# Output projection by token groups of 352, with the merging and the second norm done group by group

## Chip, core and metric

One core of one Trainium2 chip runs the whole program. The metric is the device time of one execution in microseconds (us). Three timed runs of the kernel before gave 2089.18, 2090.16 and 2091.87 us, so 2090.16 us is the median. The engines are TensorE (PE, matrix products), VectorE (DVE), ScalarE (ACT), GpSimd (POOL), and SyncE (SP), which only issues transfers (DMAs). Each engine takes its instructions in the order of its own program; they meet through semaphores.

## The reference

One step of a decoder layer with D = 1024 on 1024 prompt tokens and 8 x 4 sample tokens (1056 in all), in float32:

```python
h = rmsnorm(x, norm_mix_w) * (1.0 + sc1) + sh1
z = h @ w_in + b_in                       # 8 sections of 1024 columns
q_raw, f_raw, i_raw, og_raw, glu_a, glu_b, gate_a, gate_b = jnp.split(z, IN_SPLITS, axis=-1)
o_a, s_new = hgrn2_branch(q_raw, f_raw, i_raw, og_raw, lb, hgrn_norm_w, s0)
o_b, buf_new = conformer_conv_branch(glu_a, glu_b, buf, ...)   # ends in a layer norm and silu
merged = jnp.concatenate([sigmoid(gate_a) * o_a, sigmoid(gate_b) * o_b], axis=-1) @ w_out
x = x + g1 * merged
h2 = rmsnorm(x, norm_ffn_w) * (1.0 + sc2) + sh2
gg, uu = jnp.split(h2 @ w_ffn_in, 2, axis=-1)
x = x + g2 * ((jax.nn.silu(gg) * uu) @ w_ffn_out)
y = rmsnorm(x, norm_final_w)
```

## The kernel before

Activations lie with features on the 128 partitions and the 1056 tokens along a row: 8 feature tiles of [128, 1056]. The tokens form three groups of 352 (G = 3, GW = 352). A float32 product is made of three products of rounded parts: high x high, high x low, low x high. So each weight block of [128, 8 x 128] is loaded by SP (`load_block`, L434), rounded by ACT (`hi`, L1621), and its rest is formed by DVE or POOL (`low`, L1145 and L1888). Raw, high and low parts have two buffers each. SP may load block b when block b-2 is split (`w_split`); ACT rounds block b when PE has finished block b-2 (`block_done`).

The stages around the change:

- The last eight projection tiles (gate b, ZT + 0 to 7), each one block by three groups, 72 matmuls. Between their matmuls PE places the fills of `LAST` (five slots per tile): the recurrence of the last head, the mean of the convolution (`mu`), the token sums of its squares (`lnss`), and the layer norm's row of factors (`lnr`). ACT squares the centred tiles (L1755), POOL adds the squares up (L1998), ACT takes the root, DVE scales (L1373), ACT applies weight and bias (L1762, L1763), and DVE multiplies for the silu (L1412).
- Merging. The 16 tiles of the merged activations come back from DRAM as whole rows of 1056 tokens (`mraw`, four buffers). The eight of the second half are multiplied with the convolution's output by POOL (L2005); then ACT rounds (L1776) and DVE forms the rest (L1416). The rests lie where the projection's input lay, so they begin when the last gate tile is done.
- Output projection: 8 tiles of 128 output features, each of 2 blocks by 3 groups, 144 matmuls, 16 blocks in all. After a tile DVE adds the gated result to the residual (`tab`, two buffers, loaded by SP at L621), ACT squares the new x into the same buffer (L1826), and DVE adds the square to `ysum` (L1465).
- Second norm: token sums over all tokens (L913), root, rows, then shift and split for the first group by DVE, ACT and POOL together (L1120, L1650, L2013), and for the other two by POOL (L2023 to L2035) beside the FFN.
- FFN: for each group 22 hidden tiles of 2 blocks of 24 matmuls, then 8 output tiles of 66 matmuls.

The order in which SP issues the loads in a pair of output tiles is: residual, residual, then four weight blocks.

## Time and profile before

| | |
|---|---|
| median of three runs | 2090.16 us |
| profiled execution | 2090.47 us, span 2088.8 us |
| PE busy | 1992.8 us, 95% of the span, 15928 matmuls |
| DVE / ACT / POOL busy | 1252.0 / 659.3 / 262.4 us |
| mean granted TensorE clock | 0.974 of full speed |
| the chain that ended last | PE 86%, DVE 6%, POOL 3%, DMA 2%, ACT 2% |

A busy share is an average over stages that have different limits. The rows below are therefore taken by stage: each names a stretch, in us from the start of the span. In a timeline row the columns are the start, the duration, the engine, the line of the kernel, the operation with its tiles and shapes, the count, and in brackets how long the engine had been idle and what released it. The granted clock is a share of 2.4 GHz, so 0.50 is the lower level of 1.2 GHz.

### The profile page before, as it was taken

How to read it: one execution, taken by the hardware profiler on the slowest of the kernel's cores; microseconds unless marked ns; L12 is line 12 of the kernel's file. 1: busy time of each engine (PE TensorE's matmuls, PEld its weight loads, DVE VectorE, ACT ScalarE, POOL GpSimd, SP SyncE). 2: the span in 40 equal slices, each digit the busy share in tenths (PEclk: the TensorE clock that was granted, in tenths of full speed). 3: DMA queues.
4: the chain of work that ended last, by engine and by line, in shares of the span. 5: the costliest groups of instructions: out<-in, count | busy, mean ns of one | idle time of the engine just before them, and what ended most of it. 6: DMA issues, size and time to landing. Idle time of an engine off the chain costs nothing.

```text
span 2088.8 us, 39144 instructions
## 1 busy us (share of the span) xinstructions
PE 1992.8 (95%) x15928; PEld 1904.4 (91%) x15928; DVE 1252.0 (60%) x1667; ACT 659.3 (32%) x1001; POOL 262.4 (13%) x216
## 2 busy tenths in 40 slices
PE   7699999999999999999968997999999999999997
PEld 3599999999999999998868997999999999999997
DVE  2776979797878787876364123555445544455544
ACT  2421322222232323132452113555333333333332
POOL 0420010101010101022333222930000000000000
PEclk9799999999999999999979997999999999999998
DMA  7422222222222222222262211444444544445442
GB/s 248 159 74 55 73 75 73 75 74 76 73 75 73 76 72 76 64 81 83 73 207 93 71 61 31 133 139 140 132 141 142 149 132 137 134 142 150 140 138 91
DMA packets 368857, 220.72 MB, mean 106 GB/s; under 512 B 15208, under 2 KB 360200, under 8 KB 368705
## 3 DMA queue, kind: packets, MB, share of 16 engines
q1 hardware_dynamic: 368720, 218.77, 35.4%
q8 instruction: 102, 1.67, 0.3%
q14 instruction: 35, 0.28, 0.0%
HBM read 195.49 MB, written 24.11 MB: 105 GB/s over the span
## 4 chain that ended last, share of the span: by engine, by line
PE 86%; DVE 6%; POOL 3%; DMA 2%; ACT 2%; issue 1%; SPq 0%; DVEq 0%; ACTq 0%; POOLq 0%
PE Z L772 76%; PE R L797 2%; PE R L719 1%; PE R L850 1%; POOL mraw L2005 1%; DMA ada_w<-in_w_ada_dram 1%; PE R L803 1%; POOL ysum L1998 1%; PE R L895 1%; DVE ta L1310 1%; PE R L882 1%; PE R L875 1%; DVE x L1514 1%; DVE k L1174 1%; PE R L884 1%
## 5 line engine op out<-in xcount | busy, mean ns | idle before, releaser
L772 PE MATMUL Z<-h_hi,w_hi 128*128 128x352 f32 x2592 | 701.9, 335 | 24.0 <-POOL h_lo L1902 15.9
L772 PE MATMUL Z<-h_hi,w_lo 128*128 128x352 f32 x2592 | 675.7, 325 | 0.0
L772 PE MATMUL Z<-h_lo,w_hi 128*128 128x352 f32 x2592 | 674.5, 324 | 0.0
L1621 ACT ACTIVATE w_hi<-w_raw 128x1024 fp32r<-128x1024 f32 (+1 forms) x284 | 295.8, 1042 | 997.9 <-PE Z L772 966.9
L1145 DVE TENSOR_TENSOR w_lo<-w_raw,w_hi 128x1024 fp32r<-128x1024 f32 (+1 forms) x260 | 316.8, 1219 | 313.9 <-ACT w_hi L1621 306.2
L772 PEld LDWEIGHTS Z<-h_hi,w_hi 128*128 128x128 f32 x2592 | 455.0, 191 | 51.0 <-issue 33.5
L772 PEld LDWEIGHTS Z<-h_hi,w_lo 128*128 128x128 f32 x2592 | 465.7, 190 | 0.0
L772 PEld LDWEIGHTS Z<-h_lo,w_hi 128*128 128x128 f32 x2592 | 465.0, 190 | 0.0
L1293 DVE SCALAR_TENSOR_TENSOR yb<-up,vec,yb 128x1024 f32 (+1 forms) x240 | 308.3, 1284 | 29.8 <-DVE yb L1293 3.7
L772 PE MATMUL Z<-act_hi,w_hi 128*128 128x352 f32 x528 | 170.2, 322 | 0.0
L772 PE MATMUL Z<-act_hi,w_lo 128*128 128x352 f32 x528 | 169.5, 321 | 0.0
L772 PE MATMUL Z<-act_lo,w_hi 128*128 128x352 f32 x528 | 169.3, 321 | 0.0
L1888 POOL TENSOR_TENSOR w_lo<-w_raw,w_hi 128x1024 fp32r<-128x1024 f32 x24 | 59.2, 2468 | 373.7 <-ACT w_hi L1621 373.7
L1963 POOL TENSOR_TENSOR gate<-ta,tb 128x1056 f32<-128x1056 f32 x8 | 20.8, 2599 | 659.0 <-ACT ta L1683 659.0
L772 PEld LDWEIGHTS Z<-act_hi,w_lo 128*128 128x128 f32 x528 | 99.3, 188 | 0.0
L772 PEld LDWEIGHTS Z<-act_lo,w_hi 128*128 128x128 f32 x528 | 99.2, 188 | 0.0
L772 PEld LDWEIGHTS Z<-act_hi,w_hi 128*128 128x128 f32 x528 | 99.1, 188 | 0.0
L1545 DVE TENSOR_TENSOR tb<-ta,Z 128x352 f32<-128x352 f32 x66 | 34.4, 521 | 68.3 <-PE Z L772 67.7
L1173 DVE TENSOR_TENSOR qd<-qd,tot 128x512 f32<-128x512 f32 (+1 forms) x48 | 33.1, 690 | 43.1 <-PE R L850 41.8
L772 PE MATMUL Z<-m_hi_a,w_hi 128*128 128x352 f32 x192 | 43.5, 336 | 12.2 <-DVE m_lo_a L1416 11.8
L772 PE MATMUL Z<-m_hi_b,w_hi 128*128 128x352 f32 x192 | 43.1, 333 | 9.7 <-DVE m_lo_b L1416 9.7
L1704 ACT ACTIVATE osq<-R 128x128 f32<-128x128 f32 x80 | 21.0, 275 | 92.7 <-PE R L884 70.4
(282 smaller groups left out, 2069.8 us busy)
## 6 DMA issues: line engine op xcount, KB each, us to landing
w_raw<-in_w_ffn_in_dram SPq DMA_DIRECT2D x132, 512.0 KB, 3.8
w_raw<-in_w_in_dram SPq DMA_DIRECT2D x64, 512.0 KB, 5.0
w_raw<-in_w_ffn_out_dram SPq DMA_DIRECT2D x48, 512.0 KB, 4.1
aw<-in_w_ada_dram SPq DMA_DIRECT2D x32, 512.0 KB, 4.3
w_raw<-in_w_ffn_out_dram SPq DMA_DIRECT2D x24, 384.0 KB, 3.3
mraw<-merged_scratch SPq DMA_DIRECT2D x16, 528.0 KB, 4.3
ada_w<-in_w_ada_dram SPq DMA_DIRECT2D x8, 1024.0 KB, 7.6
w_raw<-in_w_out_dram SPq DMA_DIRECT2D x16, 512.0 KB, 4.0
```

The lines of the kernel that those rows point to most:

```text
L719: last = mm(R[n % 2][0:NSEQ, 0:2 * P], ct[:, kt, 0:NSEQ], ada_w[n % 2][:, kt, :], start=kt == 0, stop=kt == NJ - 1)
L772: last = mm(out, w[:, kt, :], x(kt, g), start=first and kt == 0 and m == 0, stop=last_block and kt == n - 1 and m == 2)
L797: return transpose(out, in_, ident[0:m, 0:m])
L803: last = mm(bank[group:group + 32, ADA_COL:ADA_COL + P], ct[:, kt, :], aw[:, kt, :], start=kt < 4, stop=kt >= 4)
L850: last = mm(bank[p:p + BAND, c * w:(c + 1) * w], k[:, t:t + BAND], halves(qd[:, t:t + BAND], 1 << lv, 1), start=True, stop=True)
L1145: st.tell(V.tensor_tensor(w_lo[b.par][:, 0:n, :], w_raw[b.par][:, 0:n, :], w_hi[b.par][:, 0:n, :].bitcast(F32), ALU.subtract), w_split, b. ...
L1173: st.do(V.tensor_tensor(late, late, pairs[:, :, 0:1].to_broadcast(shape), ALU.mult))
L1293: ins = V.scalar_tensor_tensor(yp, xp, w, yp, ALU.mult, ALU.add)
L1545: st.tell(V.tensor_tensor(a, sg, Z[t.par][:, 1, 0:GW], ALU.mult), *zfree(t))
L1621: A(w_hi[b.par][:, 0:n, :], w_raw[b.par][:, 0:n, :], ACT.Copy).then_inc(w_hi_ready, 1)
L1704: last = A(osq[:, col + i, :], bank[:, i * P:(i + 1) * P], ACT.Square, accum_out=oss[:, col + i:col + i + 1])
L1888: st.tell(Q.tensor_tensor(w_lo[b.par][:, :, :], w_raw[b.par][:, :, :], w_hi[b.par][:, :, :].bitcast(F32), ALU.subtract), w_split, b.v + 1)
```

## The change

The output projection runs group by group: 24 tiles of 48 matmuls (group outermost) instead of 8 of 144. Each group loads all 16 weight blocks again, so there are 48 blocks. DVE forms the rest of every block from the third on, POOL no longer does. Merging goes by pieces of 352 tokens: group 0 lands in free places of `x2` and is merged before the projection, groups 1 and 2 pass through seven small buffers while the tiles run (`M_AT`). The squares of a tile are added on DVE one tile later (`x2_add`), and its residual buffer is reloaded after that. The second norm's sums and rows are made per group beside the next group's tiles (for the last group beside the first FFN tiles); shift and split are POOL's for all three groups. Both roots become a power of -0.5 on POOL. The layer norm's squares start two tiles earlier, DVE adds them up instead of POOL, and scaling, affine and silu go in pieces of 352 tokens. The diff is cut to what the steps below need; what the removed lines did is told above.

```diff
-LAST = ([("rec", n) for n in range(N_LV)] + [("mu", n) for n in range(3)] + [("rec", n) for n in range(N_LV, N_OS)]
-        + [("lnss", 0)] + [("rec", N_OS)] + [("lnr", n) for n in range(3)]
-        + [("rec", n) for n in range(N_OS + 1, NFILL)])
+LAST = ([("rec", n) for n in range(N_LV)] + [("mu", n) for n in range(3)] + [("rec", n) for n in range(N_LV, N_KV0)]
+        + [("lnss", 0), ("rec", N_KV0), ("rec", N_KV1), ("lnr", 0), ("rec", N_O0), ("rec", N_O1), ("lnr", 1),
+           ("rec", N_OS), ("lnr", 2)] + [("rec", n) for n in range(N_KVS0, NFILL)])
+LAST_PAUSE = 29
...
+M2 = 2 * NJ
+MBUF = 7
+M_FIRST = (6, 7, 12, 13, 4, 5, 14, 15, 10, 11, 8, 9, 0, 1, 2, 3)
+M_AT = {0: range(16, 19), 1: range(19, 22), 2: range(22, 25), 3: range(25, 28), 4: range(28, 30), 5: range(30, 32),
+        8: range(32, 34), 9: range(34, 36), 10: range(36, 38), 11: range(38, 40), 14: range(40, 44),
+        15: range(44, 48)}
...
+    def merged_at(c):
+        g, m = divmod(c, M2)
+        raw = x2[:, M_FIRST[c] // 2, group(1 + M_FIRST[c] % 2)] if g == 0 else mbuf[(c - M2) % MBUF][:, :]
+        return raw, m_hi[m // NJ][:, m % NJ, group(g)], m_lo[m // NJ][:, m % NJ, group(g)]
+    def m_landed(c):
+        return (m_first[c], 16) if c < M2 else (m_loaded[(c - M2) % MBUF], 16 * ((c - M2) // MBUF + 1))
...
+            def load_m(c):
+                g, m = divmod(c, M2)
+                if g:
+                    wait(sp, m_split, c - MBUF + 1)
+                elif m >= NJ:
+                    sp.wait_ge(gb_stored[m % 2], 16 * ((m - NJ) // 2 + 1))
+                sp.dma_start(merged_at(c)[0], merged[m, :, group(g)]).then_inc(m_landed(c)[0], 16)
...
+                if j == 5:
+                    sp.wait_ge(m_stored, 16 * (NJ - 1))
+                    sp.wait_ge(centred, NJ)
+                    sp.wait_ge(fill_done, rec7(N_KTS).n + 1)
+                    for c in range(4):
+                        load_m(c)
...
+            def load_out(b):
+                load_block(Idx(Z_OUT + b), wout_v[:, b % 2 * 8:b % 2 * 8 + 8, b // 2 % NJ * P:(b // 2 % NJ + 1) * P])
+            def load_residual(n):
+                wait(sp, x2_summed, n - 1)
+                sp.dma_start(tab[n % 2][:, 0:GW], xt_dram[n % NJ, :, group(n // NJ)]).then_inc(xr_loaded[n % 2], 16)
+            load_out(0)
+            store_gate(5)
+            load_out(1)
             store_o(h7, rec7(N_OT2))
+            for c in (6, 8, 9):
+                load_m(c)
+            store_gate(6)
             sp.wait_ge(m_stored, 16 * NJ)
+            for c in (7, 10, 11):
+                load_m(c)
+            sp.wait_ge(ln_done, G * NJ)
+            for c in (12, 13):
+                load_m(c)
+            load_out(2)
+            load_out(3)
+            store_gate(7)
             for i in range(2):
                 sp.wait_ge(gb_stored[i], 16 * NJ // 2)
+            ahead = iter(range(M2, G * M2))
+            for c in range(MBUF):
+                load_m(next(ahead))
+            sp.wait_ge(m_prod, NJ)
+            load_residual(0)
+            load_residual(1)
+            for n in range(G * NJ):
+                if n < G * NJ - 2:
+                    load_out(2 * n + 4)
+                    load_residual(n + 2)
+                    load_out(2 * n + 5)
+                for _ in M_AT.get(n, ()):
+                    c = next(ahead, None)
+                    if c is not None:
+                        load_m(c)
...
+            def x2_fill(g, n):
+                bank = small(Idx(R_X2 + 2 * g + n))
+                if n == 0:
+                    pe.wait_ge(x2_summed, NJ * (g + 1))
+                    last = token_sums(bank, ysum[:, group(g)], GW)
+                else:
+                    pe.wait_ge(x2_recip, g + 1)
+                    last = rows_of(bank, 0, GW, rs9)
+                last.then_inc(fill_done, 1)
+            for n in range(G * NJ):
+                g, j = divmod(n, NJ)
+                pe.wait_ge(*zfree(Idx(Z_OUT + n - 2)))
                 for kk in range(2):
...
+                    beside = g and j == kk == 1 or g and j == 0 and kk == 1
+                    products(Idx(Z_OUT + 2 * n + kk), [Z[n % 2][:, 0, 0:GW]], NJ,
+                             lambda kt, _: m_hi[kk][:, kt, group(g)], lambda kt, _: m_lo[kk][:, kt, group(g)],
+                             kk == 0, kk == 1, (lambda: x2_fill(g - 1, j)) if beside else None, (5,) if beside else (),
+                             (lambda kt: pe.wait_ge(m_split, M2 * g + NJ * kk + kt + 1)) if j == 0 else None)
...
+            def add_square(j):
+                if j < 1:
+                    return
+                dve.wait_ge(ln_squared, j + 1)
                 st.settle()
...
+                st.tell(V.tensor_tensor(ysum[:, :], ysum[:, :], (v, f)[j % 2][:, :], ALU.add), ln_added, j)
...
+            after = {("rec", N_O0): (4, 0), ("rec", N_O1): (4, 0), ("rec", N_OS): (8, 0), ("lnr", 2): (0, 4),
+                     ("rec", N_KVS0): (4, 0), ("rec", N_KVS1): (4, 0), ("rec", N_OT0): (0, 4), ("rec", N_OT1): (0, 4)}
...
+            def x2_add(n):
+                dve.wait_ge(x2_squared, n + 1)
+                st.tell(V.tensor_tensor(ysum[:, group(n // NJ)], ysum[:, group(n // NJ)], tab[n % 2][:, 0:GW], ALU.add),
+                        x2_summed, n + 1)
+            dve.wait_ge(w_split, Z_OUT + 2)
+            for n in range(G * NJ):
+                g, j = divmod(n, NJ)
+                low(Idx(Z_OUT + 2 * n + 2))
+                if n:
+                    st.settle()
+                    x2_add(n - 1)
+                for c in M_AT.get(n, ()):
+                    merged_low(c)
+                low(Idx(Z_OUT + 2 * n + 3))
+                if g and j < 2:
+                    x2_evac(g - 1, j)
+                t = Idx(Z_OUT + n)
+                dve.wait_ge(block_done, Z_OUT + 2 * n + 2)
+                dve.wait_ge(xr_loaded[n % 2], (n // 2 + 1) * 16)
+                a, b = g * GW, (g + 1) * GW
+                todo = gated_add(x2[:, j, a:b], tab[n % 2][:, 0:GW], Z[n % 2][:, 0, 0:GW], G1, j, a, b)
+                for m, make in enumerate(todo):
+                    st.settle()
+                    ins = make()
+                    st.do(ins) if m < len(todo) - 1 else st.tell(ins, *zfree(t))
...
-                    act.wait_ge(*evac(Idx(REC7 + LAST_AT[("lnss", 0)])))
-                    root(NINE, ln_root)
...
+            for c in range(M2 - 2, M2):
+                merged_hi(c)
+            for n in range(G * NJ):
+                hi(Idx(Z_OUT + 2 * n + 2))
+                for c in M_AT.get(n, ()):
+                    merged_hi(c)
+                hi(Idx(Z_OUT + 2 * n + 3))
+                act.wait_ge(*zfree(Idx(Z_OUT + n)))
+                A(tab[n % 2][:, 0:GW], x2[:, n % NJ, group(n // NJ)], ACT.Square).then_inc(x2_squared, 1)
...
+                if j == 3:
+                    pool.wait_ge(*evac(Idx(REC7 + LAST_AT[("lnss", 0)])))
+                    st.do(Q.tensor_tensor(rs9[:, 0:NC], ms9[:, 0:NC], mhalf[:, 0:NC], ALU.pow))
+                    st.tell(Q.tensor_tensor(rs9[0:TS, NC:NC + 1], ms9[0:TS, NC:NC + 1], mhalf[0:TS, NC:NC + 1],
+                                            ALU.pow), ln_recip, 1)
...
+            pool.wait_ge(ln_done, G * NJ)
+            for c in range(NJ, M2 - 1):
+                gated(c)
             low(Idx(Z_OUT + 1))
...
+            gated(M2 - 1)
+            gated_group(1)
...
+            for g in range(G):
+                root(g)
+                pool.wait_ge(*evac(Idx(R_X2 + 2 * g + 1)))
...
+                if g == 0:
+                    gated_group(2)
```

## Rows read from the trace of the kernel before

**Rows 1.** The table by stage: length, busy PE, PEld, DVE, ACT, POOL; clock, DMA, GB/s

```profile
960.00:1000.00 40.00, 40.00 (x402) 38.38 (x401) 19.67 (x36) 15.80 (x27) 17.56 (x8) 1.00 0.42 134
...
1040.00:1080.00 40.00, 28.19 (x143) 26.73 (x142) 23.60 (x22) 26.09 (x24) 4.90 (x2) 0.79 0.48 162
1080.00:1120.00 40.00, 29.95 (x158) 27.32 (x157) 30.02 (x16) 11.77 (x11) 30.30 (x10) 0.91 0.54 175
...
1280.00:1320.00 40.00, 33.91 (x161) 31.54 (x161) 21.32 (x30) 18.62 (x30) 24.95 (x26) 0.68 0.23 67
```

**Rows 2.** Waits of PE, 900 to 1400: us in total, times, longest

```profile
PE Z L772 <- DVE m_lo_a L1416: 11.8, 4, 5.6
PE Z L772 <- DVE m_lo_b L1416: 9.7, 7, 2.0
PE Z L772 <- POOL h_lo L2013: 5.1, 4, 1.3
PE R L913 <- DVE ysum L1465: 4.9, 1, 4.9
PE R L913 <- POOL ysum L1998: 4.7, 1, 4.7
```

**Rows 3.** PE in slices of 5: length, busy, clock, DMA, GB/s

```profile
950.00:955.00 5.00, 2.61 (x69) 0.57 0.00 0
...
1000.00:1005.00 5.00, 0.36 (x3) 1.00 0.00 0
1005.00:1010.00 5.00, 4.93 (x23) 0.53 0.00 0
1010.00:1015.00 5.00, 5.00 (x52) 0.78 0.00 0
...
1300.00:1305.00 5.00, 5.00 (x17) 0.50 0.02 5
```

**Rows 4.** The chain that ended last: start, us, what

```profile
1110.96 163.43 PE Z L772 x1008
...
1299.94 50.16 PE Z L772 x297
```

**Rows 5.** Timeline of ACT in the FFN, two blocks in a row

```profile
1342.04 1.06 ACT L1621 ACTIVATE w_hi<-w_raw 128x1024 fp32r<-128x1024 f32 x1 [2.37 <-PE Z L772]
...
1345.85 1.06 ACT L1621 ACTIVATE w_hi<-w_raw 128x1024 fp32r<-128x1024 f32 x1 [2.40 <-PE Z L772]
```

**Rows 6.** Timeline of DVE in the same stretch

```profile
1340.46 1.27 DVE L1548 TENSOR_TENSOR act_lo<-tb,act_hi 128x352 f32 x1
1343.14 1.23 DVE L1145 TENSOR_TENSOR w_lo<-w_raw,w_hi 128x1024 fp32r<-128x1024 f32 x1 [1.40 <-ACT w_hi L1621]
```

**Rows 7.** Timeline of DVE at an FFN output tile

```profile
1491.52 0.58 DVE L1439 SCALAR_TENSOR_TENSOR x<-Z,mod,x 128x352 f32 x1 [0.34 <-DVE w_lo L1145]
1492.77 0.53 DVE L1590 TENSOR_TENSOR ysum<-ysum,tb 128x352 f32<-128x352 f32 x1 [0.67 <-ACT tb L1869]
```

**Rows 8.** Timeline of ACT at the same FFN output tile

```profile
1492.24 0.50 ACT L1869 ACTIVATE tb<-x 128x352 f32 x1 [2.32 <-DVE x L1439]
1492.67 0.85 ACT L1621 ACTIVATE w_hi<-w_raw 128x768 fp32r<-128x768 f32 x1
```

**Rows 9.** Timeline of DVE around the output projection

```profile
1055.98 1.26 DVE L1416 TENSOR_TENSOR m_lo_a<-mraw,m_hi_a 128x1056 fp32r<-128x1056 f32 x1 [5.04 <-PE Z L772]
...
1139.42 1.26 DVE L1465 TENSOR_TENSOR ysum<-ysum,tb 128x1056 f32<-128x1056 f32 x1 [1.27 <-ACT tb L1826]
```

**Rows 10.** Timeline of SP in the output projection

```profile
1140.87 0.35 SPq L621 DMA_DIRECT2D tb<-xt_scratch  x1
```

**Rows 11.** Line L434 alone, 1110 to 1290: its weight loads' time to landing

```profile
DMA to landing us min/median/max: 3.7/4.0/5.0
```

**Rows 12.** Timeline of POOL: the eight merging products, a product of 352

```profile
1080.86 25.39 POOL L2005 TENSOR_TENSOR mraw<-mraw,yb 128x1056 f32<-128x1056 f32 x8 [7.04 <-DMA mraw<-merged_scratch]
...
1301.02 0.93 POOL L2023 TENSOR_TENSOR h2buf<-x,ysum 128x352 f32<-128x352 f32 x1 [0.17 <-POOL h_lo L2013]
```

More of the change, by code:

```diff
@@ L295, in program @@
     eps = low_place("eps", [P, 1])
+    mhalf = low_place("mhalf", [P, NC + 1])
+    h2buf = low_place("h2buf", [P, GW])
     vblk = at("vblk", [TS, NS, P], F32, r.where["ktok"])
-    mraw = [at(f"mraw{i}", [P, T], F32, r.where[n]) for i, n in enumerate(("up", "gate", "tot", "O"))]
+    mbuf = [at(f"mbuf{i}", [P, GW], F32, low_place.where["otok"] + i * GW * 4) for i in range(MBUF)]
+    assert MBUF * GW * 4 <= (2 * NC + 4) * P * 4
     murow = at("murow", [P, T], F32, r.where["up"])
@@ L1383, in _ @@
                             centre(j)
-                    for j in (next(to_scale, None), next(to_scale, None)):
-                        if j is not None:
-                            scale(j)
-                    continue
-                dve.wait_ge(fill_done, fill.n + 1)
+                    if m >= N_LV:
+                        for j in (next(to_add, None),):
+                            if j is not None:
+                                add_square(j - 1)
+                else:
+                    dve.wait_ge(fill_done, fill.n + 1)
                 if kind == "mu":
@@ L1489, in x2_rows @@
-            def x2_rows(n):
-                fill = R_X2 + 1 + n
-                t0, w = ROW_PARTS[n]
-                dve.wait_ge(fill_done, fill + 1)
-                st.tell(V.tensor_copy(ysum[:, t0:t0 + w], R[fill % 2][:, 0:w]), *evac(Idx(fill)))
-            x2_rows(0)
-            st.settle()
-            for j in range(NJ):
-                wait(dve, h2_ready, j - 1)
-                modulate(tab[j % 2][:, 0:GW], x2[:, j, 0:GW], ysum[:, 0:GW], j, SH2, 0, GW, h2_full, j + 1)
-                if j in (1, 2):
-                    x2_rows(j)
+            THREE = ((P, slice(0, 2)), (GW - 2 * P, slice(2, 3)))
@@ L1815, in _ @@
-            gate_b(NJ - 1)
-            hi(Idx(Z_OUT + 1))
-            for m in range(3, 2 * NJ):
-                merged_hi(m)
-            with act.Fori(0, NJ // 2) as i:
-                for n in range(2):
-                    ft = Idx(n, i, 2)
-                    for kk in range(2):
-                        hi(Idx(Z_OUT + 2 + 2 * n + kk, i, 4))
-                    act.wait_ge(*zfree(Idx(Z_OUT + n, i, 2)))
-                    A(tab[n][:, :], at_head(x2, ft.v), ACT.Square).then_inc(x2_squared, 1)
@@ new lines, in gated, with gated_group @@
+            def gated(c):
+                g, m = divmod(c, M2)
+                j = m - NJ
+                if c < NJ + 6 or g:
+                    pool.wait_ge(*m_landed(c))
+                    gate = merged_at(c)[0]
+                else:
+                    pool.wait_ge(*zfree(Idx(ZT + j)))
+                    gate = tab[j % 2][:, 0:GW]
+                st.tell(Q.tensor_tensor(merged_at(c)[0], gate, yb[:, j, group(g)], ALU.mult), m_prod, NJ * g + j + 1)
+            def gated_group(g):
+                for j in range(NJ):
+                    gated(M2 * g + NJ + j)
```

300 lines of the change are left out of this document (107 added, 193 removed).

## The prediction

> **What bounds the kernel now.** The table by stage shows TensorE (PE) filled almost everywhere except between the last projection tiles and the FFN [rows 1]: in 1040 to 1120 it is busy 58 of 80 us at clocks of 0.79 and 0.91, and in 1280 to 1320 at 0.68. Its waits name the causes [rows 2]: 4.7 us for POOL's sums of squares of the layer norm (the norm's token sums, L913), 11.8 and 9.7 us for the low halves of the merged tiles, 4.9 and 5.1 us for the second norm. Each pause also costs clock [rows 3]: after the one that ends at 1005 the clock is 0.53, then 0.78, which loses 0.47 x 5 + 0.22 x 5 = 3.4 us. The chain of work then has one unbroken piece, 1008 matmuls in 163.4 us [rows 4], 162 ns each: the output projection, with nothing waiting. Here the change works, so this piece has to be read from the side of its feeders: how long does a weight block need to be loaded, rounded (ACT, L1621) and split (DVE, L1145), and in what order do the engines do it?
>
> One block of 24 matmuls takes 3.81 us, the distance of two roundings that wait for PE [rows 5]. A rounding starts when the block two before it is done, its product is used 1.10 us later by DVE, which takes 1.23 [rows 6]: 2.33 us from start of rounding to block ready. Call this R.
>
> **The change, part by part.**
>
> *Layer norm.* The seven adds leave POOL for DVE and the squares come two tiles earlier. The wait of 4.7 us and the 3.4 us of slow clock go: 8.1. The adds cost DVE 1.26 each (an add of that width, [rows 9]), 8.8 in all; DVE was busy only half of 960 to 1000 [rows 1], so of the bounds 0 and 8.8 I take 1. The root as a power on POOL is in no row: 8 columns, between nothing and the 3.17 us of a product of 1056 columns (25.39 / 8, [rows 12]); some 6 us of two other fills lie between the sums and its first reader, so it is hidden. Gain 7.
>
> *Start of the output projection.* Let t = 0 be the end of the last projection tile (1055.98 before, when DVE starts the first low half, [rows 9]). The normalised group 0 is ready about then, but POOL does seven products of 352 columns (3.17 / 3 = 1.06 each), then the split of block 1, then the eighth; block 1 runs at about 8 to 12. The split of block 3 stands in DVE's order behind the low halves of three tiles of group 1, and SP issues their loads only after the last gate tile is stored (about 14). So block 3 runs at about 20 and block 4 is split at about 25 (20 to 30).
>
> *Output projection.* Matmuls: the same 1152, at 3.81 / 24 = 159 instead of 162 ns. But the weights are now loaded, rounded and split three times (48 blocks instead of 16), two blocks in each 7.62 us. What was hidden before by tiles of 23 us must now fit 7.62. Follow one tile. L is the moment when block 2n+4 is split.
> 1. DVE then adds the squares of tile n: 0.03 + 0.53 = 0.56 [rows 7].
> 2. SP's next instruction is the residual load of tile n+2, which waits for that add, because it overwrites the same buffer; **the load of block 2n+5 is queued behind it**. SP starts 0.19 after the add (1139.42 + 1.26 to 1140.87, [rows 9, 10]); the residual's issue holds it about 0.40 (0.35 there).
> 3. The weight load lands 3.7 to 5.0 us after issue, median 4.0 [rows 11]; with 176 KB of residual ahead of it 4.2.
> 4. Rounding and split: R = 2.33. Block 2n+5 is ready at L + 0.56 + 0.19 + 0.40 + 4.2 + 2.33 = L + 7.68, while PE finished block 2n+4 at L + 3.81. PE is idle 3.9 us.
> 5. Only now DVE, in order, evacuates tile n+1: 0.05 + 0.58 [rows 7]. ACT, in order, squares it: 0.14 after, and takes its next rounding 0.43 later [rows 8]. That rounding is block 2n+6: again R. So block 2n+6 is split at L + 7.68 + 0.63 + 0.57 + 2.33 = L + 11.2.
>
> The period is 11.2 us for 7.62 us of matmuls. It repeats for all loads that SP queues this way: from block 4 to block 46, 21 periods, and the last tile ends 7.68 + 3.81 = 11.5 after. POOL adds to it: the second norm of groups 0 and 1 (16 steps of four operations) and 16 products now run beside this chain, some 75 us at 0.93 each [rows 12], or 7 tiles. A DVE operation of 352 columns beside POOL took 1.27 where 0.53 is normal [rows 6, 7]. Between 0 and 0.74 for each of the four DVE operations of a tile, I take 0.3: 7 x 4 x 0.3 = 8, and 2 for the two small operations per tile that the sample tokens add in the last group. Sum: 25 + 21 x 11.2 + 11.5 + 10 = 282 us. Before: 1110.96 + 163.43 - 1055.98 = 218 [rows 4, 9]. **Loss 63.**
>
> The Trainium skill (SBUF — State Buffer, the engine ports) says that a DVE operation with two SBUF inputs and a GpSimd operation exclude each other for a whole instruction. The 1.27 us beside 0.53 agrees in kind. If each of the four waited for a whole 0.93, that part would be 7 x 4 x 0.93 = 26 instead of 8, and the time 18 us longer; nothing else here uses it.
>
> *Second norm.* From the end of the projection (1274.4) to 1299.94 [rows 4] is 25.5; the slice 1300 to 1305 did 17 matmuls where 31 fit [rows 3], 2.2 more; but 21 matmuls of the first block were done in between (3.3). So 24.4 is lost today. In the new kernel groups 0 and 1 are normed beside the projection, and the last group's sums and rows (about 1.4 us of PE) beside FFN tiles. What is late next, the first FFN weights, is loaded without a residual in front. Gain 23.
>
> Sum against the profiled execution (2090.47, span 2088.8; it lies 0.3 above the median of the runs): 2090.5 - 7 + 63 - 23 = 2124.
>
> **The rivals.**
> *A, no queueing (faster).* If the odd block's load is not held up, PE never waits: 25 + 22 x 7.62 = 193 instead of 218, so -25 - 7 - 23 = -55: **2035**. For it: before, weight loads were always early. Against: the order in SP's text, and step 2 has no way round. It would need the block ready 3.9 us sooner.
> *B, half of the chain (faster).* Step 4 holds, step 5 does not, because the evacuation of tile n+1 or its square is out of the way. Then block 2n+4 is ready R after block 2n+2, and PE loses 1.2 per tile: period 8.8; 25 + 21 x 8.8 + 9 + 5 = 224, +6 - 30 = -24: **2066**. It decides from a period under 9.9, where loss and gains meet. Against: ACT and DVE take instructions in order and the new text has both in front of the next rounding.
> *C, the clock (much slower).* A pause of PE inside 950 to 955 left a clock of 0.57 [rows 3], and the new kernel has 3.9 us of pause in each tile. At half clock a block takes 7.6, which still fits into the 7.68 until the next is ready, so one slow block in two is free. If both were slow, the period would be 15.2: 25 + 21 x 15.2 + 15 + 10 = 369, +151 - 30 = +121: **2211**. Against: with both slow PE has no pause left, and the clock then comes back, as it did by 1015. The Trainium skill (TensorE: Matmul & The Clock Gate, HAM oscillation) warns of just this pattern, a wait for data before each group of matmuls and a clock that falls every time.
>
> **How the numbers follow.** Forecast 0.80: the order is in the text, the durations in rows. A 0.05, B 0.06, C 0.05, and 0.04 for other sizes around zero. The bounds of the forecast: landing 3.7, start 20, no contention: 20 + 21 x 10.7 + 11 = 256, +38 - 30 gives 2098. Landing 5.0, start 30, contention 15, adds not hidden (norm gains nothing): 30 + 21 x 12 + 12.3 + 15 = 309, +91 - 23 gives 2158. These ends would have to coincide, so the range is 2100 to 2154. A measurement of this kernel can tell about 0.2% (4 us) from no change: faster 0.11, same 0.03, slower 0.86.
>
> **What would show it.** In the new profile: PE waiting for w_lo of the odd blocks, twenty-odd times some 3.5 to 4 us; ACT's rounding waiting for the weight load there, and its even roundings waiting for DVE; tiles 11 us apart; a granted clock below 1 in the projection; no wait at the layer norm's sums and almost none before the FFN. If tiles are 7.6 apart, step 2 is wrong; if 8.8, step 5; if the projection is as forecast and the time is not, the gains are.

## The result and the profile after

The changed kernel takes 2127.85 us (median of 4 runs, 2124.66 to 2131.97); the kernel before, on the same chip, 2089.67 us (4 runs, 2088.92 to 2091.87). The ratio is 1.0193, 95% interval 1.0176 to 1.0210: slower by 1.9%. The forecast was 2124.0 in a range of 2100 to 2154. The profiled execution of after is the slowest of its four, 2131.97 us with a span of 2130.3 and a mean granted clock of 0.974.

The table by stage of after, columns as in [rows 1] (length, busy PE, PEld, DVE, ACT, POOL with the numbers of instructions, then clock, DMA share, GB/s):

```profile
960.00:1000.00 40.00, 38.29 (x313) 36.90 (x306) 26.61 (x44) 12.56 (x23) 7.18 (x4) 1.00 0.43 134
1040.00:1080.00 40.00, 26.67 (x136) 23.54 (x134) 25.61 (x32) 17.86 (x33) 14.36 (x10) 0.91 0.53 163
...
1120.00:1160.00 40.00, 31.27 (x170) 30.41 (x169) 13.55 (x18) 8.56 (x13) 0.00 (x0) 0.87 0.48 137
...
1320.00:1360.00 40.00, 33.58 (x202) 33.17 (x203) 19.01 (x31) 12.03 (x16) 1.88 (x3) 0.96 0.41 118
```

The projection, which was the unbroken piece of [rows 4], now has PE busy 31 of 40 us (1120 to 1160), while every feeder is idle more than half of that stretch. Nobody is full: a sign of a chain of waits. The waits of PE from 900 to 1400 (total, times, longest; compare [rows 2]):

```profile
PE Z L804 <- DVE w_lo L1174: 68.2, 24, 5.5
PE Z L804 <- DVE m_lo_a L1422: 4.7, 7, 2.2
```

Neither the layer norm's sums nor the second norm appears any more; the low halves of weight blocks do, some once per tile. Who keeps them late (waits of SP's queue and of ACT, 1070 to 1360):

```profile
SPq L642 <- DVE ysum L1506: 211.0, 22, 12.4
...
ACT w_hi L1655 <- DMA w_raw<-in_w_out_dram: 133.5, 21, 8.7
```

SP stands 211 us in front of the residual load (L642). One tile, from the chain of work that ended last, 1153 to 1166 (start, us, what):

```profile
1153.40 1.24 DVE w_lo L1174
...
1154.66 0.54 DVE ysum L1506
...
1155.21 0.34 SPq L642
...
1155.59 4.22 DMA w_raw<-in_w_out_dram
...
1159.84 1.07 ACT w_hi L1655
...
1160.93 1.23 DVE w_lo L1174
...
1162.42 0.59 DVE x L1476
...
1163.44 1.05 ACT w_hi L1655
...
1164.52 1.24 DVE w_lo L1174
```

This is the prediction's chain, step by step: split of the even block, add (0.54), residual issue, landing 4.22, rounding and split, evacuation, rounding and split. From one even block's split to the next it is 11.12 us (1153.40 to 1164.52), forecast 11.2; the odd block is 7.53 after the even one (1160.93), forecast 7.68.

The whole difference of the two profiled executions, 41.5 us, splits at three moments. The first is DVE's first write of the convolution's mean (`murow`: before at 934.51, after at 930.00). The second is DVE's first low half of the merged tiles [rows 9], in after:

```profile
1043.22 8.85 DVE L1422 TENSOR_TENSOR m_lo_a<-x,m_hi_a 128x352 fp32r<-128x352 f32 x8 [0.18 <-ACT m_hi_a L1813]
```

The third is the end of the projection, 1274.39 before [rows 4] and 1339.90 after, where the FFN's first product follows the projection's last on PE without a gap:

```profile
1339.90 0.32 PE L804 MATMUL Z<-h_hi,w_hi 128*128 128x352 f32 x1
```

| stretch | before | after | difference | forecast |
|---|---|---|---|---|
| start to mean of the convolution | 934.5 | 930.0 | -4.5 | 0 |
| mean to first low half (gate tiles, layer norm) | 121.5 | 113.2 | -8.3 | -7 |
| output projection | 218.4 | 296.7 | +78.3 | +63 |
| end of projection to end of span | 814.4 | 790.4 | -24.0 | -23 |

The first line holds no work that the change touches. In the twelve kernels of the experiments below, which differ from after only behind it, the moment lies between 929.4 and 933.1, so 3.7 us are the variation of single executions. All of them, and after, lie below the 934.5 of before, of which there is one trace; whether the rest is chance is not shown.

### The profile page after: what moved, and what is told of

Same layout as the page of the kernel before. It is cut to its first block, busy times and chain, and to the rows that moved or that the text cites. A ratio compares the mean times of both kernels' runs of the same rounds, so it can differ in the third digit from the quotient of the medians.

```text
span 2130.3 us, 39297 instructions
## 1 busy us (share of the span) xinstructions
PE 1994.4 (94%) x15928; PEld 1904.9 (89%) x15928; DVE 1312.2 (62%) x1792; ACT 666.3 (31%) x1070; POOL 237.3 (11%) x244
## 4 chain that ended last, share of the span: by engine, by line
PE 77%; DVE 10%; DMA 6%; ACT 3%; issue 1%; SPq 1%; POOL 0%; DVEq 0%; ACTq 0%
PE Z L804 67%; DMA w_raw<-in_w_out_dram 4%; DVE w_lo L1174 3%; ACT w_hi L1655 2%; PE R L829 1%; PE R L882 1%; PE R L751 1%; DMA ada_w<-in_w_ada_dram 1%; PE R L835 1%; PE R L927 1%; DVE ta L1339 1%; PE R L907 1%; PE R L914 1%; DVE ysum L1506 1%; DVE k L1203 1%
## 5 line engine op out<-in xcount | busy, mean ns | idle before, releaser
L1174 DVE TENSOR_TENSOR w_lo<-w_raw,w_hi 128x1024 fp32r<-128x1024 f32 (+1 forms) x306 | 379.4, 1240 | 468.4 <-ACT w_hi L1655 459.8
L1655 ACT ACTIVATE w_hi<-w_raw 128x1024 fp32r<-128x1024 f32 (+1 forms) x316 | 329.2, 1042 | 1025.3 <-PE Z L804 876.7
L804 PE MATMUL Z<-m_hi_b,w_hi 128*128 128x352 f32 x192 | 76.6, 399 | 69.9 <-DVE w_lo L1174 66.8
L804 PEld LDWEIGHTS Z<-m_hi_b,w_hi 128*128 128x128 f32 x192 | 45.3, 236 | 76.7 <-DVE w_lo L1174 73.3
L804 PE MATMUL Z<-m_lo_b,w_hi 128*128 128x352 f32 x192 | 72.8, 379 | 0.0
L804 PE MATMUL Z<-m_hi_b,w_lo 128*128 128x352 f32 x192 | 72.3, 377 | 0.0
L804 PE MATMUL Z<-m_hi_a,w_hi 128*128 128x352 f32 x192 | 62.9, 328 | 6.1 <-DVE m_lo_a L1422 4.7
```

What stands on the lines that cost most here:

```text
L804: last = mm(out, w[:, kt, :], x(kt, g), start=first and kt == 0 and m == 0, stop=last_block and kt == n - 1 and m == 2)
L1174: st.tell(V.tensor_tensor(w_lo[b.par][:, 0:n, :], w_raw[b.par][:, 0:n, :], w_hi[b.par][:, 0:n, :].bitcast(F32), ALU.subtract), w_split, b. ...
L1655: A(w_hi[b.par][:, 0:n, :], w_raw[b.par][:, 0:n, :], ACT.Copy).then_inc(w_hi_ready, 1)
```

## The experiments

In all that follows the *period* is the distance from the end of one even block's split by DVE to the end of the next, over the 21 periods from block 4 to block 46. In after it is 12.0 us in the mean, 10.9 to 11.3 in the ten shortest. Diffs are against the kernel after unless said otherwise.

### Is it the queue behind the residual, and which steps of the chain count?

The first four ran together (the kernel before took 2086.71 us there).

**e1: the odd block's load ahead of the residual.**

```diff
                     load_out(2 * n + 4)
-                    load_residual(n + 2)
                     load_out(2 * n + 5)
+                    load_residual(n + 2)
```

> The changed kernel with two lines of SP's program exchanged: the odd weight block of a tile is loaded before the residual, not behind it. Theory (the residual's wait holds the load up, and with it the whole chain): the 23 waits of PE for w_lo of the odd blocks, 65.8 us, go, the 21 tile periods fall from a mean of 12.0 to about 7.7 us, and the time falls by some 90 us, to 2030 to 2045. Rival 1 (three times the weight traffic, DVE and POOL in each other's way, or the lowered clock limits the projection): the work and its neighbours are the same, so the time stays within 5 us of 2128. Rival 2 (only the odd block is late): as the theory, since its load is freed.

Measured: 2071.52 us (2070.44 to 2073.93), ratio to before 0.9924 (0.9907 to 0.9940). So 56 us faster than after, faster than before, and yet 26 us or more above what I expected. The odd block now follows the even one after 2.3 us in the last four tiles, but the mean period is 9.4, not 7.6. The timeline of SP, two tiles:

```profile
1085.46 0.34 SPq L642 DMA_DIRECT2D tb<-xt_scratch  x1
1085.85 1.38 SPq L604 DMA_DIRECT2D mbuf<-merged_scratch  x3
1087.27 1.30 SPq L459 DMA_DIRECT2D w_raw<-in_w_out_dram  x2
1095.72 0.34 SPq L642 DMA_DIRECT2D ta<-xt_scratch  x1
```

After 1087.27 + 1.30 SP issues nothing for 7 us and stands before the residual (132.2 us in 22 waits over the stretch). The wait did not go, it only has other things queued behind it: the merged tiles and then the even block, whose rounding now waits for its landing:

```profile
1092.82 1.06 ACT L1655 ACTIVATE w_hi<-w_raw 128x1024 fp32r<-128x1024 f32 x1 [3.70 <-DMA w_raw<-in_w_out_dram]
```

**e2: ACT squares tile n after the rounding of block 2n+4** instead of before it (this takes step 5 out).

```diff
                 hi(Idx(Z_OUT + 2 * n + 2))
+                if n:
+                    x2_square(n - 1)
                 for c in M_AT.get(n, ()):
                     merged_hi(c)
                 hi(Idx(Z_OUT + 2 * n + 3))
-                act.wait_ge(*zfree(Idx(Z_OUT + n)))
-                A(tab[n % 2][:, 0:GW], x2[:, n % NJ, group(n // NJ)], ACT.Square).then_inc(x2_squared, 1)
```

> The changed kernel with ACT's square of tile n moved behind the rounding of block 2n+4 (one rounding later than now); SP's order is unchanged. It tests step 5 of the prediction alone: the square and the evacuation before it are then off the way to the next even block. Theory: the odd block is still 7.5 us behind the even one, but the even one is again ready R = 2.3 us after PE leaves block 2n+2: period 8.7 to 8.9 instead of 10.9 where POOL is quiet, in all 2.1 x 21 = 44 us less, 2078 to 2090. If the full chain of step 5 isn't what sets the period: no change, 2128.

Measured: 2103.73 us (2099.38 to 2104.51), ratio 1.0075 (1.0057 to 1.0093), the period 10.7 in the mean and 9.8 to 10.1 in the seven shortest, where 8.7 to 8.9 were expected. ACT's timeline:

```profile
1154.49 1.06 ACT L1655 ACTIVATE w_hi<-w_raw 128x1024 fp32r<-128x1024 f32 x1 [5.64 <-DMA w_raw<-in_w_out_dram]
1156.00 1.06 ACT L1655 ACTIVATE w_hi<-w_raw 128x1024 fp32r<-128x1024 f32 x1 [0.45 <-DMA w_raw<-in_w_out_dram]
```

Both blocks of a pair now wait for their landing (38 waits, 150.3 us, where after has 21). The even block 2n+6 is issued right behind the odd block 2n+5 and thus behind the same wait for the add; it lands 1.5 us after it here, 2.4 in the next tile, where two merged loads stand between the two. In after that second transfer was hidden by step 5. So the period has two nearly equal ways round, and taking one away uncovers the other. My price for rival B (8.8) had only the first of them.

**e3: DVE adds the squares before it splits the even block** (step 1 moves off the path).

```diff
-                low(Idx(Z_OUT + 2 * n + 2))
                 if n:
                     st.settle()
                     x2_add(n - 1)
+                low(Idx(Z_OUT + 2 * n + 2))
```

> The changed kernel with DVE's add of tile n moved ahead of the split of block 2n+4; SP's order is unchanged. It tests step 2, what the residual waits for: the add then comes right after the square of tile n. Chain now: split of block 2n+3, evacuation 0.63, square 0.64, add 0.57, SP 0.59, load 4.2, R 2.33, which makes 9.0 us from odd block to odd block, instead of 10.9: 40 us less, 2082 to 2095. If PE or the weight traffic sets the period: no change.

Measured: 2069.56 us (2066.12 to 2070.63), ratio 0.9912 (0.9896 to 0.9929); the period is 9.2 in the mean (9.0 expected) after 12.0: it fell by more than the 2.2 us that the chain alone would give. Half of the excess is in the odd block's load, which lands after 4.17 us in the mean on the chain of this trace and after 4.48 in after's; the longest tiles shrank most (13.0 to 14.2 in after, at most 10.8 here). Why the load lands sooner is not shown. Two lines in DVE's program, exchanged, are worth 58 us and turn the loss into a gain:

```profile
1143.25 0.53 DVE L1506 TENSOR_TENSOR ysum<-ysum,ta 128x352 f32<-128x352 f32 x1 [0.63 <-ACT ta L1867]
1144.13 1.23 DVE L1174 TENSOR_TENSOR w_lo<-w_raw,w_hi 128x1024 fp32r<-128x1024 f32 x1 [0.35 <-ACT w_hi L1655]
```

The add ends at 1143.78 and SP issues the residual at 1143.80, when the split has not begun; in after the add came behind it.

**e4: three idle copies, 0.90 us together, ahead of the add**, to lengthen step 1.

```diff
                 if n:
+                    for _ in range(3):
+                        st.settle()
+                        st.do(V.tensor_copy(attc[:, 1:NC, :], attc[:, 1:NC, :]))
                     st.settle()
                     x2_add(n - 1)
```

> The changed kernel with three extra copies of 224 columns on DVE (a buffer that nobody reads) just ahead of the add of tile n, some 0.4 us each. DVE is busy less than half of this stage, so by the rivals (traffic, clock) they cost nothing or little, 2128 to 2133. Theory: they stand in the chain, once a tile, so each tile grows by their whole 1.2 us: 21 x 1.2 = 25, 2148 to 2160.

Measured: 2153.06 us (2151.11 to 2155.37), ratio 1.0320 (1.0303 to 1.0337). The period is 12.99 instead of 12.01: 0.98 for copies that take 0.94 with their gap (0.3 us each, where 0.4 was expected). Over 21 periods that is 20.6 us; the two profiled executions are 19.3 apart, the medians 25.2. What stands between the split and the add is paid in full in every tile, which is what a chain through every tile means.

### Is the wait the whole of it?

The next four ran together (the kernel before: 2090.71 us).

**e5: the residual one tile later**, when its buffer should be free before SP comes to it.

```diff
             load_residual(0)
-            load_residual(1)
             for n in range(G * NJ):
                 if n < G * NJ - 2:
                     load_out(2 * n + 4)
-                    load_residual(n + 2)
+                if n < G * NJ - 1:
+                    load_residual(n + 1)
+                if n < G * NJ - 2:
                     load_out(2 * n + 5)
```

> The kernel after with the residual of each output tile loaded one tile later, so that SP's wait for the buffer that it overwrites is over before SP reaches it, and nothing is queued behind a wait: both w_out blocks and the merged loads go out when their buffers are free. My theory (the queue behind the residual's wait is the whole chain from one tile to the next): the period of a tile falls from 12.0 to the 7.6 us of its matmuls plus up to 0.6, the 21 periods take 160 to 172 us instead of 252, and the time is 2035 to 2055. Rival, the length of the period is the traffic and the vector engine's own load beside GpSimd: then two blocks wanted at once still land late, the period stays at 9 or more, and the time is 2070 or more, as in e1 and e3.

Measured: 2046.54 us (2045.75 to 2049.55), ratio 0.9799 (0.9774 to 0.9824): 81 us faster than after, 2% faster than before. SP's waits and those of PE:

```profile
SPq L459 <- DVE w_lo L1175: 128.1, 43, 8.6
SPq L642 <- DVE ysum L1507: 7.3, 21, 0.8
...
PE Z L805 <- DVE w_lo L1175: 9.3, 6, 4.5
```

SP waits now for free weight buffers (L459), as it should, and 7.3 us instead of 211 for the add. The table by stage shows PE full in the first stretch below, although the feeders and the transfers have more to do in each 40 us than in after (182 GB/s against 137); the second holds the one long tile:

```profile
1120.00:1160.00 40.00, 39.72 (x252) 39.46 (x251) 24.69 (x30) 15.57 (x23) 16.00 (x16) 1.00 0.59 182
1160.00:1200.00 40.00, 35.31 (x207) 34.75 (x206) 24.14 (x27) 15.36 (x22) 28.95 (x27) 0.91 0.50 150
```

The mean period is 8.25; without one tile of 13.1 it is 8.0. The time from issue to landing of the weight loads (L459), after from 1070 to 1330, then e5 from 1070 to 1250:

```profile
DMA to landing us min/median/max: 4.0/5.1/6.1
```

```profile
DMA to landing us min/median/max: 3.7/4.0/5.6
```

The same loads land 1.1 us sooner in the median, though more bytes move per us: in after SP releases them in pairs, as the end of its wait lets them go, in e5 one by one as buffers come free. But 1.1 us is small beside what is gained: the loads are issued early enough that ACT waits 5.8 us for them in e5 and 132.0 in after. The same traffic, and the same work of DVE beside POOL, now fit into 173 us instead of 252. That rules out the rival (traffic, or DVE's load beside POOL) as the main cause.

**e6: the start loosened too** (diff against e5, the lines that matter; the tiles of group 1 in `M_AT` move from n = 0 to 5 to n = 2 to 7).

```diff
             load_out(2)
-            load_out(3)
             store_gate(7)
+            load_out(3)
...
-            for c in range(NJ, M2 - 1):
+            for c in range(NJ, NJ + 4):
                 gated(c)
             low(Idx(Z_OUT + 1))
-            gated(M2 - 1)
+            for c in range(NJ + 4, M2):
+                gated(c)
```

> e5 with the start of the projection loosened too: SyncE stores gate tile 7 ahead of the third w_out block, GpSimd and ScalarE split the second half of the w_out buffers' first use earlier, and the merged tiles of group 1 are built two to seven tiles later with their loads behind a w_out block. By my theory the start (block 4 split at 30.6 us after the last gate tile in the kernel after, 25 forecast) is the queue of SyncE again: that falls to 22 to 26 and the time is 5 to 8 us below e5's. Rival, the start is bound by the merging of group 0 and nothing of this matters: within 2 us of e5.

Measured: 2043.04 us (2040.34 to 2048.30), ratio 0.9787 (0.9757 to 0.9817). Block 4 is split 25.3 us after the first low half (1042.63 to 1067.9), against 30.3 in e5 and 30.6 in after: that term does what was expected of it. The time, 3.5 us below e5 where 5 to 8 were expected, is not told apart from e5 by the intervals. In after SP's timeline shows what held the start:

```profile
1045.92 10.38 SPq L459 DMA_DIRECT2D w_raw<-in_w_out_dram  x2
1056.35 0.58 SPq L635 DMA_DIRECT2D merged_scratch<-tb  x1
1061.68 3.19 SPq L604 DMA_DIRECT2D mbuf<-merged_scratch  x7
```

The load of block 3 waits until 1055.92 for its buffer, which POOL frees with the split of block 1 (1053.25, 2.66 us); the store of the last gate tile is queued behind it, and all seven merged loads wait for that store to land. It is the same pattern once more.

**e7b: POOL's work in the second norm cut to half.**

```diff
                     sec = SH2 * NJ + j
+                    if g < 2:
+                        st.do(Q.tensor_copy(h2_hi[:, j, a:b], x2[:, j, a:b]))
+                        st.settle()
+                        st.tell(Q.tensor_copy(h2_lo[:, j, a:b], x2[:, j, a:b]), h2_ready, NJ * g + j + 1)
+                        continue
                     st.settle()
                     st.do(Q.tensor_tensor(h2buf[:, :], x2[:, j, a:b], ysum[:, a:b], ALU.mult))
```

> The kernel after, with GpSimd's four operations per tile of the second norm, in groups 0 and 1, replaced by two plain copies (so the FFN of these two groups works on x2 without its norm and its output is another). It measures the contention between VectorE and GpSimd, which I put at 8 us and the trace shows larger. My theory (VectorE's operations on the chain, the split and the add, are slower while GpSimd works): the periods of tiles 9 to 13 and 17 to 22 fall from 12.6 to 14 to about 11 to 12, and the time is 10 to 14 us below the kernel after, 2114 to 2118. Rival, these tiles are long because of the transfers of the merged weights in the same tiles: no change, 2126 to 2130.

Measured: 2123.59 us (2122.69 to 2125.00), ratio 1.0172 (1.0146 to 1.0197), 4 us below after where 10 to 14 were expected, and the intervals overlap; the two profiled executions are 9.3 us apart. The traces tell more. DVE's operations in the projection, after first, then e7b (busy, mean ns, idle before):

```profile
L1174 DVE TENSOR_TENSOR w_lo<-w_raw,w_hi 128x1024 fp32r<-128x1024 f32 x42 | 58.2, 1385 | 141.1 <-ACT w_hi L1655 141.1
...
L1506 DVE TENSOR_TENSOR ysum<-ysum,tb 128x352 f32<-128x352 f32 x10 | 7.1, 714 | 0.3
```

```profile
L1174 DVE TENSOR_TENSOR w_lo<-w_raw,w_hi 128x1024 fp32r<-128x1024 f32 x43 | 55.4, 1288 | 141.9 <-ACT w_hi L1655 141.9
...
L1506 DVE TENSOR_TENSOR ysum<-ysum,tb 128x352 f32<-128x352 f32 x11 | 6.1, 554 | 0.4
```

The splits are 0.15 us longer in after than their normal 1.24, the adds about 0.13 longer than 0.53: 42 x 0.145 + 21 x 0.13 = 9 us of contention in after, and 2 to 3 in e7b. The mean period falls from 12.0 to 11.6, 9.0 us over the 21. So contention exists in the size that the prediction gave it (8). It also made the long tiles where POOL works at the norm: the three periods between 1177.7 and 1216.8, 13.4, 12.6 and 13.1 us in after, are 11.4, 11.3 and 11.5 in e7b, with the same merged loads in them, which speaks against the rival. I had expected too much of the time, because POOL's remaining work still lengthens 8 of 43 splits in e7b, and two periods stay long (13.3 and 12.7); in the first of them the chain runs through the load of a merged tile (4.62 us) and its product on POOL.

**e8: the layer norm's adds back on POOL**, at their earlier places.

```diff
-                        for j in (next(to_add, None),):
-                            if j is not None:
-                                add_square(j - 1)
+                        next(to_add, None)
...
+                if j in (2, 3):
+                    for n in range(1, 6) if j == 2 else range(6, NJ):
+                        pool.wait_ge(ln_squared, n + 1)
+                        if n > 1:
+                            pool.wait_ge(ln_added, n - 1)
+                        st.tell(Q.tensor_tensor(ysum[:, :], ysum[:, :], (v, f)[n % 2][:, :], ALU.add), ln_added, n)
```

> The kernel after, with the token sums of the layer norm accumulated on GpSimd as before the change. The gate stage gained 8.3 us by the trace, forecast 7, and I put that down to the adds' move to VectorE and the order by group. If the move of the adds is what gained it, the matmuls wait for the sums again and the time is 4 to 8 us above the kernel after, 2131 to 2136. If the order by group alone did it, no change, 2126 to 2130.

Measured: 2130.89 us (2129.67 to 2133.77), ratio 1.0209 (1.0182 to 1.0235), overlapping with after's. The trace decides it: the sums on PE have no wait, although POOL adds.

```profile
981.32 2.46 POOL L2034 TENSOR_TENSOR ysum<-ysum,f 128x1056 f32<-128x1056 f32 x1
...
984.61 1.99 PE L945 MATMUL R<-ones,ysum 128*128 128x1 f32 x18
```

POOL is done at 983.8, 0.8 us ahead. From the mean of the convolution to the first low half it is 114.9 us here (931.74 to 1046.64), 113.2 in after and 121.5 before. So some 6.6 of the 8.3 us of this stage do not come from the move of the adds, which is worth at most the remaining 1.7 (executions differ by as much). The squares' earlier place explains why the wait is gone: POOL's first add starts at 954.14 here and started at 982.56 before. e8 keeps the new order of the fills, the power and the pieces of 352 too, and what each of these is worth is not shown.

### What is left, and a better kernel

In e5 and e6 one tile stays long (13.1 and 12.1 us). POOL makes the eight products of group 2 only after the whole norm of group 0, though their data is there:

```profile
1173.02 8.70 POOL L2049 TENSOR_TENSOR mbuf<-mbuf,yb 128x352 f32<-128x352 f32 x7
1185.25 0.94 POOL L2049 TENSOR_TENSOR mbuf<-mbuf,yb 128x352 f32<-128x352 f32 x1 [3.53 <-DMA mbuf<-merged_scratch]
```

**e9: these products before the norm** (against e6; the kernel before ran at 2088.43 us beside e9 and e10).

```diff
             for g in range(G):
                 root(g)
+                if g == 0:
+                    gated_group(2)
...
-                if g == 0:
-                    gated_group(2)
```

> e6 with one order changed on GpSimd: the eight products of group 2 before the second norm of group 0 instead of behind it. In e5 and e6 one tile is long, 13.1 and 12.1 us, where these products come at 1181 although their data landed before, because GpSimd works through 32 operations of the norm first; VectorE and ScalarE wait for them in order ahead of the weight block of the next tile. Theory: that tile falls to about 8.5 and the time is 3 to 5 us below e6, 2037 to 2041. Rival, the norm is now late for the FFN or the next groups, or this pause only moves: 2043 or more.

Measured: 2057.39 us (2055.74 to 2060.01), ratio 0.9852 (0.9832 to 0.9872): 14 us slower than e6. The long tile is gone, as expected (7.7 us after 12.1), and a tile of 26.6 us has come:

```profile
1181.39 1.29 POOL L2049 TENSOR_TENSOR mbuf<-mbuf,yb 128x352 f32<-128x352 f32 x1 [20.12 <-DMA mbuf<-merged_scratch]
...
1213.96 0.71 POOL L2067 TENSOR_TENSOR rs<-ms,mhalf 128x2 f32<-128x2 f32 x1
```

```profile
1215.34 1.56 PE L846 MATMUL R<-ident,rs 128*128 128x128 f32 x6 [15.86 <-POOL rs L2068]
```

POOL waited 20 us for the load of the eighth tile, whose buffer is free only when tile 14 splits the first, so the norm of group 0 ran 1183 to 1214, the root of group 1 came behind it, and PE, whose order is fixed, stood 15.9 us before the fill that reads it. The rival was right.

**e10: e9 with the order of e3.**

> e9 with the order of e3 too: VectorE adds the squares of the last tile before it splits the next even block. In the kernel after this alone was worth 58 us, because SyncE waited for it. If the queue behind SyncE's wait was all there was to gain from it, it is worth nothing once that wait is gone: within 2 us of e9. Rival, the add's place costs VectorE's own order time: 3 us or more below e9.

Measured: 2052.29 us (2050.64 to 2055.75), ratio 0.9827 (0.9809 to 0.9844), 5 us below e9; the runs hardly meet, the intervals of the ratios overlap. The 21 periods together are only 1.9 us shorter (185.7 to 183.8).

**e11: seven of the products between the sixth and seventh tile of the norm, the eighth behind it** (against e6; the kernel before: 2087.03 us).

```diff
+                    if g == 0 and j == 5:
+                        for i in range(NJ - 1):
+                            gated(M2 * 2 + NJ + i)
                 if g == 0:
-                    gated_group(2)
+                    gated(M2 * 3 - 1)
```

> e6 with seven of GpSimd's eight products of group 2 put between the sixth and the seventh tile of the second norm of group 0, where their data has just landed, and the eighth behind the norm as it was: GpSimd's order is changed, but it waits nowhere longer. e9 showed that with the products first GpSimd sits 20 us in a wait for the eighth tile's load and then computes the root of group 1 so late that the matmuls that read it, fixed in TensorE's order, wait 15.9 us. Theory: the long tile (12.1 us in e6) falls to some 9, the root stays on time, and the time is 2 to 5 us below e6, 2038 to 2041. Rival, the long tile is the price of the merged tiles themselves and comes back elsewhere: 2042 to 2046.

**e12: e11 with the order of e3.**

> e11 with VectorE's add ahead of its split of the even block, as in e3. e10 against e9 gave 5 us where 0 to 2 were expected, at the edge of what the two intervals tell apart. If the add's place is worth something even where no load waits for it, this is 3 to 6 us below e11; if that was chance, within 2 us.

Measured: e11 2042.30 us (2036.79 to 2043.85), ratio 0.9776 (0.9749 to 0.9803); e12 2038.50 us (2035.34 to 2042.03), ratio 0.9760 (0.9733 to 0.9787). The long tile falls from 12.1 to 9.3 and the mean period from 8.35 to 8.18, so the mechanism holds; the time is not told apart from e6. The add's place gave 5.1 and 3.8 us in the two pairs, the same sign twice, but neither pair alone shows it, and in the second the 21 periods give 0.9 of it; that stays open. e12 is the fastest kernel here: 2.4% under the kernel before and 4.2% under the change as made. All that PE still waits there for weight blocks, 900 to 1400:

```profile
PE Z L806 <- DVE w_lo L1176: 3.1, 2, 2.5
```

## Why the prediction was right, point by point

**The chain (steps 1 to 4).** Right in its terms in the tile shown above, which has no work of POOL beside it: add 0.54 (0.56 forecast), residual issue 0.34 with its gap (0.40), landing 4.22 (4.2), 7.53 from even to odd (7.68). SP's reaction was too dear, 0.02 instead of 0.19: in the place of [rows 9, 10] SP runs two register instructions (0.06 and 0.03 us, L621) between its wait and the issue, and none at L642 in after. The gap before the evacuation I took as 0.05, where [rows 7] has 0.34; it is 0.13 in after (1151.18 to 1151.31). e4 shows that a delay there is paid one to one, e3 that the order of two DVE operations decides it, and e5 that without SP's wait nothing of it is left.

**Step 5 and the period.** Right in the sum, 10.9 to 11.3 in ten of 21 tiles (11.2). It is not the only way round, as the prediction had it: e2 shows the landing of the next even block, 1 us behind it.

**The start.** 30.6 instead of 25, outside my 20 to 30 by a little. Failed step: I had SP load the merged tiles of group 1 after the last store at about 14 us. The store is issued at 13.1 after the first low half (1056.35), but the loads then wait for it to land, 5.3 us (1061.68). I followed the issue of a transfer and forgot its landing. e6 gets 5 us of this term back.

**The sum of periods and the end.** 252.2 us over 21 periods where 235.2 + 10 was forecast, so 7 were missing from it. Contention was well sized (9 against 8). The term sized too small is the landing: 19 loads of odd blocks on the chain of after take 4.48 us in the mean (3.96 to 5.51) instead of 4.2, 5.3 us in all. The merged loads behind them are not the reason: with some queued behind it a block lands after 4.47 (9 loads), without after 4.49 (10). In one period (13.0, from 1238.8) the chain leaves the weight load and goes through the load of a merged tile (4.32) and its product on POOL (0.94), and DVE reads the second norm's sums ahead of two evacuations and its rows ahead of two more, 1.2 us on the chain; neither had a price in the prediction. SP's faster reaction gave some 3.5 back. The last tile took 13.8 (1326.1 to 1339.9) instead of 11.5: its last load landed after 5.08, and PE took 5.4 for the last block instead of 3.81, part of it at the lower clock (0.72 in 1335 to 1340).

**The rule on the engine ports.** The splits and adds, with two inputs in SBUF, became longer beside POOL, the evacuation, which reads one of its two tiles from PSUM, did not. POOL's timeline in after, then DVE's at the same time:

```profile
1091.90 3.74 POOL L2047 TENSOR_TENSOR mbuf<-mbuf,yb 128x352 f32<-128x352 f32 x3 [8.32 <-DMA mbuf<-merged_scratch]
```

```profile
1092.32 1.60 DVE L1174 TENSOR_TENSOR w_lo<-w_raw,w_hi 128x1024 fp32r<-128x1024 f32 x1 [4.22 <-ACT w_hi L1655]
1094.06 0.58 DVE L1476 SCALAR_TENSOR_TENSOR x<-Z,mod,ta 128x352 f32<-128x352 f32 x1
```

Over the projection, 28 of 42 splits meet no operation of POOL and take 1.22 to 1.23; 14 overlap one, and 13 of these take 1.48 to 1.96. Of 21 adds 16 are alone (0.53) and 5 beside POOL (0.85 to 1.16). Of 21 evacuations 12 are beside POOL and take what the others take. The Trainium skill (SBUF — State Buffer, SBUF: two separate sides) names on VectorE's side the operations with two SBUF inputs (beside a faster mode of others), and the trace agrees. Taken as a whole POOL operation of waiting each time it would have made 26 us; measured are 9, because two thirds of the splits and three quarters of the adds come while POOL does nothing. A split was at most 0.7 us longer.

**Layer norm.** -8.3 against -7, and no cost of the adds to be seen. The reason was half right: the wait went, and with the squares earlier it is gone with the adds on POOL too (e8); their move to DVE was not needed.

**Second norm.** -24.0 against -23. Nothing took its place; in 1320 to 1360 the FFN follows the projection at once.

**The rivals.** A (2035) did not come, since SP's text had the wait; but e5, e6, e11 and e12, which take the wait away, reach 2047 to 2038, so its price was right within 0.6%. Part of that is luck too: of the 25 us that A gave to the projection, e5 gains 6.7 and e12 14.5, and the traces reach the changed part 3.0 and 4.6 us before that of the kernel before. B's order of things exists, its period of 8.8 doesn't, for the reason in e2. C, the clock, is there and costs little. PE in slices of 5 us in after, one pause and what follows:

```profile
1145.00:1150.00 5.00, 1.86 (x12) 1.00 0.78 211
1150.00:1155.00 5.00, 3.77 (x13) 0.50 0.01 2
1155.00:1160.00 5.00, 5.00 (x30) 0.82 0.75 211
1160.00:1165.00 5.00, 5.00 (x32) 1.00 0.13 37
```

After a slice with 3.1 us of pause the clock is at the lower level, and back in the slice after the next. The Trainium skill (TensorE: Matmul & The Clock Gate, HAM oscillation) warns of this, and the trace agrees that it happens. But the slow part falls where PE would wait for the odd block anyway: the tile from 1153.40 to 1164.52 takes 11.12 us, as if the clock had never fallen. In two places of after the slow matmuls were on the chain: at the last block, and in the tile below, with a granted clock of 0.66 in 1105 to 1110, where 48 matmuls took 9.52 us instead of 7.62. Together that is at most 3.5 us.

```profile
1105.31 9.52 PE Z L804 x48
```

In e5, almost without pauses, the clock is 1.00 from 1120 to 1160.

That the total came within 4 us of the median rests in part on luck: the projection was 15 us dearer than forecast, the profiled execution reached the changed part 4.5 us early and gained 2 us more on both sides, and the median lies 4 us under the profiled execution.

## What to carry to other kernels

When weights are streamed, look in the transfer engine's own list of waits for a transfer that has to wait for a computation: all that stands behind it in the queue inherits its wait, and merely moving it behind one load gives the wait to the next (e1), while issuing it one step later, when its buffer is free, removes it (e5). Reloading the weights three times was then hidden in this kernel: the projection takes 211.7 us in e5 (1046.33 to 1258.0) and 203.9 in e12 (1043.21 to 1247.1), against 218.4 before. And before moving work on an engine with a fixed order, ask what that engine will wait for in its new place, and who reads what stands behind it (e9).

## What the runs showed of the hardware that I had not expected

- Two weight loads of 512 KB issued one right after the other land 1.5 us apart (e2: the roundings that they release start at 1154.49 and 1156.00). Released in pairs by a wait (after) they land after 5.1 us in the median, issued one by one (e5) after 4.0, although the queue moves more bytes per us there.
- A power on POOL has its price by the column. In after 128x8 took 1.66 us, 128x2 0.71 and 96x1 0.56, where a product of 352 columns takes 0.93. An estimate from these three sizes is 0.4 us and 0.16 for each column:

```profile
983.48 1.66 POOL L2033 TENSOR_TENSOR rs<-ms,mhalf 128x8 f32<-128x8 f32 x1 [13.12 <-DVE ms L1451]
```

- SP reacts to DVE's semaphore in 0.02 us and issues the next transfer behind a finished wait 0.38 after it (the add ends at 1155.20, the issues start at 1155.21 and 1155.59).
